# Page compression in a decoder step: dense weights in two column halves, adjacent moving columns, page numbers loaded sixteen at a time

## What is computed

```python
def compress(x_raw, pe, w):
    B, Tk = x_raw.shape[:2]
    xb = x_raw.reshape(B, Tk // CMP_BLOCK, CMP_BLOCK, N_KV, HEAD_DIM) + pe[:, None, :]
    return jnp.einsum('bnlgd,lde->bnge', xb, w)
...
    k = rmsnorm(compress(kc_raw, pe[0], w[0]), k_norm_c)
    v = compress(vc_raw, pe[1], w[1])
```

## Time and profile before

| | us |
|---|---|
| median of three timed executions | 5335.08 |
| lowest and highest of them | 5327.94, 5337.42 |
| profiled execution: its span, first to last instruction | 5330.7 |
| of it, `compress`, from its first DMA issue to the first of the next stage | 811.9 to 1388.1 |

### The profile page before, as it was taken

The page is one execution under the profiler, slowest core; times in us unless marked ns, Lnnn a source line. Parts: engine busy times, 40 slices in busy tenths (PEclk is TensorE's granted clock), DMA queues, the critical chain, the costliest instruction groups (busy, mean ns, idle before and its releaser), DMA issues. The chain is left out here.

```text
span 5330.7 us, 69054 instructions
## 1 busy us (share of the span) xinstructions
PE 4885.4 (92%) x24624; PEld 4169.7 (78%) x24624; DVE 1182.2 (22%) x2834; ACT 866.9 (16%) x1552; POOL 203.6 (4%) x200
## 2 busy tenths in 40 slices
PE   7898896999588989989964899999999999999999
PEld 6787785999366867767754788888888888888888
DVE  3334320000454444433420100011001110021001
ACT  0101100000144444544420000011000100011000
POOL 0000000000121110100100000000000000000000
PEclk9999996999688999999975899999999999999999
DMA  3001006444100000000012232223222232222221
GB/s 141 11 34 44 14 14 188 145 144 139 39 16 13 10 11 9 8 11 7 8 40 56 102 108 75 75 91 103 75 75 75 87 108 76 78 91 72 75 75 64
DMA packets 222450, 348.01 MB, mean 65 GB/s; under 512 B 49347, under 2 KB 149500, under 8 KB 221349
## 3 DMA queue, kind: packets, MB, share of 16 engines
q1 hardware_dynamic: 170700, 295.96, 17.3%
q10 hardware_dynamic: 50105, 39.60, 2.6%
q0 software_dynamic: 1440, 9.62, 0.5%
HBM read 313.28 MB, written 36.56 MB: 66 GB/s over the span
## 5 line engine op out<-in xcount | busy, mean ns | idle before, releaser
L1475 PE MATMUL ps_t<-h_normed,w_ring 128*128 128x257 f32 x5120 | 1116.6, 379 | 1.4
L1475 PEld LDWEIGHTS ps_t<-h_normed,w_ring 128*128 128x128 f32 x5120 | 964.4, 189 | 152.3 <-DVE h_normed L1565 10.0
L1453 PE MATMUL ps_t<-ff,w_ring 128*128 128x257 f32 x4096 | 889.1, 379 | 2.8 <-ACT ff L1543 2.8
L1453 PEld LDWEIGHTS ps_t<-ff,w_ring 128*128 128x128 f32 x4096 | 772.8, 189 | 119.0 <-ACT ff L1543 4.4
L246 PE MATMUL ps_z<-a_chunk,w_in_sb 128*128 128x257 f32 x2816 | 624.3, 383 | 50.0 <-DVE a_chunk L284 31.8
L246 PEld LDWEIGHTS ps_z<-a_chunk,w_in_sb 128*128 128x128 f32 x2816 | 537.4, 191 | 133.0 <-DVE a_chunk L284 33.0
L464 PE MATMUL ps_cmp<-pages,w_cmp_sb 128*128 128x128 f32 (+1 forms) x2176 | 465.2, 391 | 10.4 <-DMA pages<-in_cache_cmp 10.4
L464 PEld LDWEIGHTS ps_cmp<-pages,w_cmp_sb 128*128 128x128 f32 x2176 | 436.9, 206 | 38.6 <-DMA pages<-in_cache_cmp 10.5
L842 ACT ACTIVATE PT_pr<-ps_p 128x512 f32<-128x512 f32 (+1 forms) x576 | 312.0, 542 | 533.8 <-PE ps_p L747 493.9
L731 PE MATMUL ps_s<-ks_pr,q_sel_pr 128*128 128x512 f32 (+2 forms) x832 | 320.4, 511 | 16.8 <-DVE chunk_max_pr L952 16.8
L772 PE MATMUL ps_o<-vs_pr,PT_pr 128*128 128x64 f32 x2560 | 321.0, 269 | 0.0
(11 more groups left out here) (249 smaller groups left out, 3370.8 us busy)
## 6 DMA issues: line engine op xcount, KB each, us to landing
w_ring<-in_w_tail SPq DMA_DIRECT2D x328, 512.0 KB, 3.5
pages<-in_cache_cmp ACTq DMA_DIRECT2D x256, 128.0 KB, 3.9
pages<-in_cache_cmp SPq DMA_DIRECT2D x256, 128.0 KB, 4.0
w_in_sb<-in_w_in SPq DMA_DIRECT2D x22, 512.0 KB
x_chunk<-in_xT SPq DMA_DIRECT2D x4, 2056.0 KB
mix_chunk<-scratch_mixT SPq DMA_DIRECT2D x4, 2056.0 KB
x_chunk_t<-in_xT SPq DMA_DIRECT2D x4, 2056.0 KB
out_yT<-h SPq DMA_DIRECT2D x32, 257.0 KB
```

What stands on the lines that cost most here:

```text
L1453: mm = pe.matmul(zp[zi][:, hh, 0:HF], w[:, i], src[:, k, hh * HF:(hh + 1) * HF], start=(first and i == 0), stop=(final and i == len(ks) - ...
L1475: mm = pe.matmul(zp[(m + 1) % 3][:, hh, 0:HF], w[:, k], a[:, k, hh * HF:(hh + 1) * HF], start=(k == 0), stop=(k == KT - 1), skip_group_che ...
```

## The change

In `compress`:

- **Layout of pages and weights.** The 128 partitions of a page buffer now hold two neighbouring tokens x 64 channels of one head. The two heads are side by side in the columns. A call contracts two tokens at once, with a weight of 128 x 64 without zeros, so 16 calls replace 32 for keys, and 16 for values. Keys go to output partitions 0 to 63 and values to 64 to 127, call by call in turn. The moving operand is `pg[b][:, :, kv, j]`: for each of 32 pages, 8 neighbouring columns (two heads x four blocks), 256 in all.
- **Page numbers.** `values_load_multi_w_load_instructions` reads up to 16 page numbers at a time. The loops are written out. SP loads pages 0 to 19 of a chunk (16, then 4), ACT pages 20 to 31; the page's place in the buffer is constant.
- **Normalizing and transposing** are done per chunk while the next is in work (`after`, `rooted`, `norm`). A chunk is taken out by one DVE instruction instead of two.
- **The prompt's part** moves between chunk 3 and chunk 4: SP loads it into a tile of its own after chunk 1's pages, and TensorE runs 128 calls with weights of 64 x 64 and 64 columns, every 32nd. Its sum and its transpose come after chunk 4.
- **Order at the start.** The page table is loaded first; the weights (1 MB, and 1 MB with the two token halves swapped, `wx`) are loaded whole, so GpSimd's clearing goes. `line` is computed after chunk 0 instead of first of all, and the bias band follows it.

In `sample`, each of the 16 calls becomes two, one per head, with keys of 64 partitions.

The diff, cut to its core:

```diff
+    MID, SPLIT = 3, 20
-        wc = sb("w_cmp_sb", [128, 2, CB, 128])
+        wc, wx = sb("w_cmp_sb", [128, 2, CB // 2, HD]), sb("w_cmp_crossed", [128, 2, CB // 2, HD])
-        pg = [sb(f"pages{b}", [128, NPG, 2, PAGE]) for b in range(2)]
+        pg = [sb(f"pages{b}", [128, NPG, 2, CB // 2, 8]) for b in range(2)]
...
+        def load_pages(eng, which, ci, lo, hi):
+            b, i = ci % 2, ci // 2
+            if i:
+                eng.wait_ge(s_done[b], ONE + i)
+            for x0 in range(lo, hi, 16):
+                n = min(16, hi - x0)
+                a = NPG * ci + x0
+                _, pages = nc.values_load_multi_w_load_instructions(
+                    ptab[0:1, a:a + n], engines=[which], min_val=0, max_val=d["cache_cmp"].shape[0] - 1)
+                for x, page in enumerate(pages):
+                    eng.dma_start(pg[b][:, x0 + x].rearrange("p k j n -> p (k j n)"),
+                                  d["cache_cmp"][ds(page, 1)].rearrange("a p n -> (a p) n")).then_inc(s_pg[b], 16)
...
             def _(sp):
+                sp.dma_start(ptab[:], d["page_table"]).then_inc(s_c, 16)
+                sp.dma_start(wc[:], d["w_cmp"][0]).then_inc(s_w, 16)
+                for a, b in ((pe_t, "cmp_pe"), (gk, "k_norm_cmp")):
                     sp.dma_start(a[:], d[b]).then_inc(s_c, 16)
+                sp.dma_start(wx[:], d["w_cmp"][1]).then_inc(s_w, 16)
                 sp.wait_ge(s_c, ONE + 48)
+                for ci in range(NCH):
+                    load_pages(sp, mybir.EngineType.SP, ci, 0, SPLIT)
+                    if ci == 1:
+                        sp.dma_start(kvp[:], d["kvT"][0:2, :, 0:SEQ].rearrange("k p n -> p k n")).then_inc(s_pr, 16)
...
+                def chunk(ci):
+                    b, i = ci % 2, ci // 2
+                    pe.wait_ge(s_pg[b], ONE + 16 * NPG * (i + 1))
+                    pe.wait_ge(s_ev[b], ONE + i)
+                    for j in range(CB // 2):
+                        for kv in range(2):
+                            mm = pe.matmul(cps[b][HD * kv:HD * kv + HD, 0:2 * NBL], wc[:, kv, j], pg[b][:, :, kv, j],
+                                           start=(j == 0), stop=(j == CB // 2 - 1))
+                    mm.then_inc(s_done[b], 1)
+                def after(ci):
+                    b, i = ci % 2, ci // 2
+                    pe.wait_ge(s_ev[b], ONE + i + 1)
+                    pe.wait_ge(s_te, ONE + ci)
+                    for g in range(2):
+                        mm = pe.transpose(tps[:, g, 0:HD], kvc[64:128, g, NBL * ci:NBL * ci + NBL], t["ident"][64:128, 64:128])
+                    mm.then_inc(s_tr, 1)
+                    pe.wait_ge(s_sq, ONE + ci + 1)
+                    pe.wait_ge(s_rt, ONE + ci)
+                    pe.matmul(sps[0:64, 0:2 * NBL], t["ones_hd"][0:64, 0:64],
+                              sq[0:64, b].rearrange("p g n -> p (g n)"), start=True, stop=True).then_inc(s_sum, 1)
...
+                for ci in range(NCH):
+                    chunk(ci)
+                    if ci == 0:
+                        pe.wait_ge(s_ri, 32)
+                        for i, (a, n) in enumerate(line_parts):
+                            if i == 2:
+                                pe.wait_ge(s_line, 1)
+                            pe.matmul(lps[:, i % 2, 0:n], relb[:], oneh[:, a:a + n], start=True, stop=True).then_inc(s_lm, 1)
+                        pe.wait_ge(s_cvd, ONE + 1)
+                    if ci:
+                        after(ci - 1)
+                    if ci == MID:
+                        pe.wait_ge(s_pr, ONE + 16)
+                        for j in range(CB // 2):
+                            for odd in range(2):
+                                for kv in range(2):
+                                    for g in range(2):
+                                        o = HD * (kv ^ g)
+                                        mm = pe.matmul(pps[g][o:o + HD, 0:NCP], (wx if odd ^ g else wc)[HD * g:HD * g + HD, kv, j],
+                                                       kvp[HD * g:HD * g + HD, kv, 2 * j + odd::CB],
+                                                       start=(j == 0 and not odd), stop=(j == CB // 2 - 1 and odd == 1))
+                        mm.then_inc(s_pd, 1)
...
             def _(act):
+                for ci in range(2):
+                    load_pages(act, mybir.EngineType.Activation, ci, SPLIT, NPG)
+                for ci in range(NCH):
+                    if ci + 2 < NCH:
+                        load_pages(act, mybir.EngineType.Activation, ci + 2, SPLIT, NPG)
+                    rooted(ci)
+                    if ci == MID - 1:
+                        act.wait_ge(s_pk, ONE + 4)
+                        act.activation(kvp[:, 0, 0:NCP], kp[:], ACT.Square).then_inc(s_p2, 1)
...
@@ sample
-                        a = NCP + 256 * b + 128 * y
-                        mm = pe.matmul(psS[:, y, NH * b:NH * b + NH], t["kcT"][:, a:a + 128], qz[:, :, b], start=True, stop=True)
+                        for g in range(2):
+                            a, c0 = 256 * b + 128 * y, NH * b + 4 * g
+                            mm = pe.matmul(psS[:, y, c0:c0 + 4], t["kvc"][0:64, g, a:a + 128], qs[:, g, :, b], start=True, stop=True)
```

More of the change, by code:

```diff
@@ L350, in compress @@
     NPG = 32
-    plain = t["plain"]
+    NCH = NB * NPAGE // NPG
+    NBL = NPG * PAGE // CB
+    MID, SPLIT = 3, 20
     with ExitStack() as ctx:
@@ L367, in compress @@
         cmask = sb("cmask", [128, BANDW])
-        lps = pb("ps_line", [NH, 3, 512])
+        lps = pb("ps_line", [NH, 2, 512])
         line_parts = ((0, 512), (512, 512), (1024, 128))
[L370 to L375, removed]
+        s_w, s_c, s_cv, s_cvd, s_pr, s_pd, s_pk, s_p2, s_pn, s_kz = (sem(n) for n in (
+            "weights_loaded", "consts_loaded", "pe_summed", "pe_copied", "prompt_loaded", "prompt_summed",
+            "prompt_copied", "prompt_rooted", "prompt_normed", "prompt_kept"))
+        s_sq, s_sum, s_rt, s_rc, s_kn, s_tr, s_te = (sem(n) for n in (
+            "squared", "squares_summed", "root", "reciprocal", "k_normed", "v_transposed", "v_copied"))
         s_pg, s_done, s_ev = ([sem(f"{n}{b}") for b in range(2)] for n in ("pages", "chunk_summed", "chunk_copied"))
@@ new lines, in _ @@
+            @block.tensor
+            def _(pe):
+                def chunk(ci):
[18 more added lines that the diff above has]
+                              sq[0:64, b].rearrange("p g n -> p (g n)"), start=True, stop=True).then_inc(s_sum, 1)
+                pe.wait_ge(s_w, ONE + 32)
+                pe.wait_ge(s_c, ONE + 48)
+                for x in range(2):
+                    for j in range(CB // 2):
+                        for kv in range(2):
+                            o = HD * (kv ^ x)
+                            mm = pe.matmul(sps[o:o + HD, x:x + 1], wc[:, kv, j], pe_t[:, kv, j:j + 1], start=(j == 0),
+                                           stop=(j == CB // 2 - 1))
+                mm.then_inc(s_cv, 1)
+                for ci in range(NCH):
[11 more added lines that the diff above has]
+                        pe.wait_ge(s_pr, ONE + 16)
+                        for j in range(CB // 2):
+                            for odd in range(2):
+                                for kv in range(2):
+                                    for g in range(2):
[4 more added lines that the diff above has]
+                        mm.then_inc(s_pd, 1)
+                    if ci == MID + 1:
+                        pe.wait_ge(s_pk, ONE + 4)
+                        pe.wait_ge(s_p2, ONE + 1)
+                        pe.matmul(pps[0][:, 0:NCP], t["ones_hd"][:], kvp[:, 0, 0:NCP], start=True, stop=True).then_inc(s_pd, 1)
+                        pe.transpose(pps[1][0:NCP, 0:128], vp[:], t["ident"][:]).then_inc(s_pd, 1)
+                after(NCH - 1)
@@ L435, in _ @@
             @block.scalar
             def _(act):
-                act.wait_ge(s_c, ONE + 48)
[L438 to L447, removed]
@@ new lines, in norm @@
+                def norm(ci):
+                    b = ci % 2
+                    dve.wait_ge(s_rt, ONE + ci + 1)
+                    dve.reciprocal(rt[0:64, b], rt[0:64, b]).then_inc(s_rc, 1)
+                    dve.wait_ge(s_rc, ONE + ci + 1)
+                    k = kvc[0:64, :, NBL * ci:NBL * ci + NBL]
+                    dve.scalar_tensor_tensor(k, k, gk[0:64, 0:1], rt[0:64, b], ALU.mult, ALU.mult).then_inc(s_kn, 1)
+                for g in range(2):
+                    dve.memset(t["kcz"][HD - HD * g:2 * HD - HD * g, g], 0.0).then_inc(s_kz, 1)
@@ L501, in _ @@
                 dve.wait_ge(s_cvd, ONE + 1)
-                def copy(b, a, n):
-                    dve.tensor_scalar(kcT[:, a], cps[b][:, 0:n], cvec[:, 0:1], None, ALU.add).then_inc(s_k0, 1)
-                    dve.tensor_scalar(vcT[:, a], cps[b][:, 128:128 + n], cvec[:, 1:2], None, ALU.add).then_inc(s_ev[b], 1)
-                with dve.Fori(0, NCH // 2) as i:
-                    for b in range(2):
```

(2 more changed lines are left out.)

172 lines of the change are left out of this document (67 added, 105 removed).

## The result

The changed kernel takes **5100.9 us** (median of four runs, 5097.9 to 5101.4) beside 5334.0 for the kernel before: a ratio of 0.9563 [0.9552, 0.9575]. The profiled execution has a span of 5096.0 us.

The account below looks back on a forecast made before the run. SP's queue was to bound `compress`, 16.8 us a chunk against TensorE's 15.0: 6 + 269 + 6 + 26 + 6 + 22 + 1 = 336 us against 576, 7 more in `sample`, so 5102 us (chance 0.36), range 5005 to 5185.

Parts of the forecast that it names:

- rival B: TensorE's chunks in `compress`: keys' and values' halves run side by side, 7 us a chunk; 5070 us, down to 5010; chance 0.34.
- SP's queue sets the pace: Page loading in `compress`: 0.84 us a page, 16.8 us for SP's 20 pages, 269 us for 16 chunks.
- Rival C: SP's page numbers stay dear, each paying its own load: 1.11 us a page, 22.2 for 20; 5175 us; chance 0.17.
- TensorE's chunk: Matmuls of a chunk: 64 records at 0.216 us, 13.8 us, 15.0 with `after`, priced like 257 neighbouring columns.
- The stops, 6: SP's waits: 3 us for chunk 0's buffer before chunk 2, 3 more for `line` and DVE's copies.
- the prompt, 26: The prompt's part in mid-stream: 256 records at 114 ns, 29 us, while SP stops; 26 after TensorE's slack.
- The band, 6: `skew` and `band` loading during chunks 1 to 4: 24 us of transfers, cost 0 to 24, taken as 6.
- Start and end: Ends of the `compress` stage: 6 us until first page numbers; last chunk 22 and barrier 1 at the end.
- D: Runs of 8 columns in `compress` are paid as strided, 440 ns a record; 5302 us; chance 0.07.
- E: TensorE's array empties between column halves in `compress`, 474 ns a record; slower, 5406 us; chance 0.06.
- The sample stage: Compressed keys times queries in `sample`: 32 more records at 0.214 us each, 7 us more.

Follow-up runs that it names:

- one_number: The changed kernel with page numbers loaded one at a time instead of up to 16 at a time: 5167.2 us, ratio 0.9687.
- halves_apart: The changed kernel with all 16 calls for keys before all 16 for values, instead of in turn: 5126.5 us, ratio 0.9612.
- band_spread: The changed kernel with `skew` and `band` moved head by head, one head in each chunk from the second on: 5077.1 us, ratio 0.9520.
- strided_apart: The changed kernel with a call's columns 32 apart and all keys before all values: 5272.5 us, ratio 0.9884.
- strided: The changed kernel with pages laid out so that a call's 256 columns lie 32 apart, keys and values in turn: 5118.0 us, ratio 0.9590.
- no_range_check: The changed kernel without the range check of each page number: 5046.0 us, ratio 0.9459.

## Why the prediction was right, and where it was not

The time was predicted at 5102 and came at 5100.9. The bound is the one that was named, SP's queue. That the number is so close is luck: TensorE went as rival B had it, which asks for 5070, and a band of 20 us instead of 6, a slower pace and longer stages elsewhere made up the difference.

**SP's queue sets the pace: right.** 0.84 us a page was predicted, 0.856 measured (17.1/20): a number costs 0.31 with its share of the load instead of 0.29, an issue 0.515 instead of 0.55 with its register work. 16 chunks make 274 us against 269. Rival C falls by the 973 ns load; one_number prices what it would have cost, 66 us where I had 73.

**TensorE's chunk: wrong.** The step "I take the 257-column row, the nearest in columns" put 216 ns on a record and 13.8 us on a chunk; it took 7.1. For TensorE rival B was right. The Trainium skill's rule behind it (TensorEngine Tiling (Array Packing), Key Properties: tiles work independently) agrees with this trace: 7.13 us in turn, 13.2 apart. halves_apart has the chunks of the forecast, and it took 5126, 26 more than the changed kernel. B's own sum had SP's queue as the bound too: 6 + 269 + 13 + 16 = 304 for the stage, where the last chunk is 7 shorter. The measured 327 has 5 more in the pace, 16 more in SP's stops, most of it the band's, and 2 at the end; with 7 us in the prompt's stages that is the way from 5070 to 5101.

**The stops, 6, and the prompt, 26: nothing.** SP did not wait for chunk 0's buffer, and its one wait, 3.4 us for the late chunk 2, was over at 913.6, before the prompt's records began at 925.5. "29 us in the middle of the stream" is the step that failed: the 256 records took 8.5 us, four quarters of the array in turn, where the earlier trace rows show the whole array, one record after another.

**The band, 6: wrong the other way.** "0 to 24, taken as 6" was 20 by SP's queue (28.6 us lost against 8.7 in band_spread), 19 by the stage and 24 by the time. The step that failed is "four chunks leave over 4 us each": SP stands in its issues while the DMA engines are full, and it doesn't make up the time, since it has no slack against itself. Before the change `skew` and `band` took as long to land, but SP then waited 107.7 us for chunks, room enough to make up a stop.

**Start and end.** SP loaded its first page numbers at 818.6, 6 us into the stage, as forecast. From there 15 paces of 17.1 would bring those of chunk 15 at 1075, and they came at 1103.7: 29 lost, where stops, prompt and band were 38. After chunk 15's 17.1 us 18 remain to the end; 23 were forecast. 6 + 274 + 29 + 18 = 327 against 6 + 269 + 38 + 23 = 336.

**Rivals D and E fall.** 64 records with runs of 8 neighbours cost 13.2 us in halves_apart, 206 ns each, and 26.05 us with the step of 32 in strided_apart, 407 each; in the changed kernel a record costs 111. So no pace came to D's 440 or E's 474. The trace agrees with the 16-byte lines of the Trainium skill (SBUF — State Buffer, Door 1: The DMA port swizzle) as far as these two layouts go.

**The sample stage** needed 7 us more, as forecast: its multiplication of compressed keys and queries, before and after.

```profile
2762.52 6.99 PE L1190 MATMUL ps_sT<-q_padded,kcT_sb 128*128 128x8 f32 x32 [27.77 <-DMA new_kw<-out_kvT]
```

```profile
2520.36 13.81 PE L1233 MATMUL ps_sT<-q_groups,kvc_sb 64*128 64x4 f32 x64 [27.76 <-DMA new_kw<-out_kvT]
```

The prompt's stages, untouched, took 7 us longer (1358.3 against 1351.3): from the stage's 249.5 us less, a net 235 remain; forecast 233.

## To carry to other kernels

When a change takes a stage off one engine, work out who is next in line and price every edit against that one: here each of two speedups of TensorE alone came within 17 to 26 us of both together, and 0.25 us of register work a page on a queue was worth 55. A queue that sets the pace can't make up a stop, so bulk transfers beside it belong in small pieces where the DMA engines have room; spread like that, they cost SP's queue 20 us less here. Ask which cover a hidden transfer has, and whether the change moves the cover away.

## What the runs showed that was not expected

- A load of page numbers into registers was cheap in fours: 297 ns for 4 page numbers, 784 for 12, 973 for 16, but 268 for 1, 475 for 2, 678 for 3, 2833 for 13 and 3028 for 14. By these durations the splits of 18 and 19 pages lost to the loads much of what they moved off SP. The loads of 13 and 14 also began at another place in the table, so only for 2 and 3 is it shown that the count alone is the cause.
- DMA engines 0.99 busy moved 314 GB/s with 1 KB rows, and 361 while `skew` and `band` took part (366 with those cut to 2 KB pieces).
- The strided stream took the same time at a lower granted clock. In strided, chunks 0 and 1 took 14.0 us each at 0.84 and at 1.00; in halves_apart, with neighbouring columns, chunks 0 and 1 took 15.7 us at 0.84 and 13.2 at 1.00.
- The prompt's stages, the same instructions in every kernel, took 1349 to 1367 us. Windows over them, one_number and then no_range_check:

```profile
1210.90:2560.10 1349.20, 1203.52 (x7696) 961.17 (x7696) 582.18 (x2075) 616.41 (x1173) 189.84 (x181) 0.92 0.05 13
```

```profile
1079.90:2446.60 1366.70, 1221.58 (x7696) 977.81 (x7696) 582.20 (x2075) 616.46 (x1173) 189.87 (x181) 0.91 0.05 13
```

The same 7696 records kept TensorE busy 18 us longer at a granted clock of 0.91 instead of 0.92, and the other engines not at all. Why the clock differed was not tried. Differences of under 10 us between whole runs should be read from the stage's own windows.
